# Query projections and attention in one program: gate of three tiles from resident tokens, sampled tokens' attention spread over the chunks

## The reference

```
groups: (window, dilation) = (128, 1), (512, 4), (2048, 16)
query t reads positions t - k*d, k = 0..window/d, that are >= 0
s = q . k * SCALE;  lse = logsumexp(s);  o = exp(s - lse) @ v        per group and head
o = sum over groups of softmax(lses)[group] * o[group]
x = x + RMSNorm_post((o * silu(z)) @ w_out)
```

## Time and profile before

| what | value |
|---|---|
| median of 3 runs | 2730.37 us |
| the profiled execution, its own time | 2728.19 us |
| its span, first to last instruction | 2726.1 us |
| mean granted TensorE clock | 0.969 |
| PE busy | 2594.7 us (95%) |
| DVE, ACT, POOL busy | 1138.7, 856.0, 540.5 us |
| last query matmul starts | 1823.57 us |
| first matmul of the sampled tokens starts | 1851.78 us |
| first score matmul of the prompt starts | 1926.80 us |

### The profile page before, as it was taken

One profiled execution on the slowest core, in us unless ns is written; L12 is line 12 of the kernel. 1 busy time (PEld: TensorE's weight loads), 2 busy tenths in 40 slices (PEclk: granted clock), 3 DMA queues, 4 the chain that ended last, 5 costly groups with the idle time before them and its releaser, 6 DMA issues. The chain is left out here.

```text
span 2726.1 us, 38145 instructions
## 1 busy us (share of the span) xinstructions
PE 2594.7 (95%) x14140; PEld 2379.5 (87%) x14140; DVE 1138.7 (42%) x2431; ACT 856.0 (31%) x2109; POOL 540.5 (20%) x577
## 2 busy tenths in 40 slices
PE   6999999999999979999999999977899999899997
PEld 5999999999988757778999999976799899788885
DVE  7311112111144433211434545431455665677774
ACT  6211111111145432100000000003466666666662
POOL 1010101010012211111222222220222122233332
PEclk9999999999999989999999999995799999899999
DMA  4323333232365543873445455445566565544441
GB/s 156 96 81 96 99 106 93 83 115 94 124 198 186 173 156 125 250 213 110 101 114 119 115 119 120 113 93 165 185 243 236 199 214 193 200 137 152 152 152 64
DMA packets 303428, 391.12 MB, mean 143 GB/s; under 512 B 79261, under 2 KB 228405, under 8 KB 301770
## 3 DMA queue, kind: packets, MB, share of 16 engines
q1 hardware_dynamic: 297114, 345.55, 41.5%
q10 hardware_dynamic: 6192, 44.01, 5.0%
HBM read 269.84 MB, written 163.68 MB: 159 GB/s over the span
## 5 line engine op out<-in xcount | busy, mean ns | idle before, releaser
L281 PE MATMUL a_pair<-a_ht_hi,a_w_hi 128*128 128x412 f32 (+1 forms) x1280 | 448.7, 351 | 2.0 <-DVE a_ht_lo L450 2.0
L282 PE MATMUL a_pair<-a_ht_lo,a_w_hi 128*128 128x412 f32 (+1 forms) x1280 | 447.8, 350 | 0.0
L283 PE MATMUL a_pair<-a_ht_hi,a_w_lo 128*128 128x412 f32 (+1 forms) x1280 | 447.8, 350 | 0.0
L1121 PE MATMUL p_pair<-p_ht_lo,p_q_hi 128*128 128x416 f32 (+1 forms) x960 | 335.5, 350 | 0.0
L1120 PE MATMUL p_pair<-p_ht_hi,p_q_hi 128*128 128x416 f32 (+1 forms) x960 | 335.5, 349 | 0.0
L1122 PE MATMUL p_pair<-p_ht_hi,p_q_lo 128*128 128x416 f32 (+1 forms) x960 | 334.3, 348 | 0.0
L281 PEld LDWEIGHTS a_pair<-a_ht_hi,a_w_hi 128*128 128x128 f32 x1280 | 241.5, 189 | 3.0 <-DVE a_ht_lo L450 2.4
L282 PEld LDWEIGHTS a_pair<-a_ht_lo,a_w_hi 128*128 128x128 f32 x1280 | 241.2, 188 | 1.0
L283 PEld LDWEIGHTS a_pair<-a_ht_hi,a_w_lo 128*128 128x128 f32 x1280 | 241.1, 188 | 0.6
L1304 POOL TENSOR_TENSOR p_q_out<-p_q_out,p_turned 128x416 f32<-128x416 f32 (+1 forms) x120 | 139.3, 1177 | 399.7 <-DVE p_turned L1251 325.8
L1249 DVE TENSOR_TENSOR p_q_out<-p_pair,p_table 128x416 f32<-128x416 f32 (+1 forms) x120 | 93.0, 775 | 293.8 <-PE p_pair L1122 173.9
(11 more groups left out here) (217 smaller groups left out, 5173.7 us busy)
## 6 DMA issues: line engine op xcount, KB each, us to landing
out_cache_kv_g_sample<-cache_kv_g ACTq DMA_DIRECT2D x72, 410.0 KB, 3.6
p_table<-rope_columns SPq DMA_DIRECT2D x60, 416.0 KB, 3.2
scratch_q_tiles<-p_q_out SPq DMA_DIRECT2D x48, 512.0 KB, 5.7
g_q_raw<-scratch_q_tiles SPq DMA_DIRECT2D x48, 512.0 KB, 3.9
scratch_partial<-g_parts SPq DMA_DIRECT2D x32, 520.0 KB, 4.7
g_parts<-scratch_partial SPq DMA_DIRECT2D x32, 520.0 KB, 6.4
a_w_raw<-a_w_in SPq DMA_DIRECT2D x32, 512.0 KB, 6.5
g_rows_hi<-scratch_ht_tiles SPq DMA_DIRECT2D x32, 512.0 KB, 5.6
```

The source lines that it names most:

```text
L281: nc.tensor.matmul(out, hi, ht_hi[:, k, cols], start=(k == 0), stop=False)
L282: nc.tensor.matmul(out, hi, ht_lo[:, k, cols], start=False, stop=False)
L283: last = nc.tensor.matmul(out, lo, ht_hi[:, k, cols], start=False, stop=(k == KT - 1))
L1121: nc.tensor.matmul(out, hi, ht_lo[:, k, cols], start=False, stop=False)
```

## The change

Blocks 2, 3 and 4 become one. `attention_phase` turns into `attention_programs`, which returns pieces that `projection_phase` puts behind its own on each engine; `sample_attention_phase` is gone. In detail:

- The query pairs run from group 2 to group 0 (`q_group`), so the tiles that attention takes first are stored first.
- The first half of the gate weights is loaded and split during the last pair: SP loads slices 0 to 3 ahead of the pair's tables and 4 to 7 between them, ACT makes the high parts, and DVE makes two low parts ahead of each of the first four rotations. The first of these loads waits until the store of pair 10 has landed.
- The gate jobs 0 to 2 (Z_FIRST = 3) read the resident ht_hi and ht_lo and stand right behind the last query job on PE; the turns of keys 0 and 1 stand ahead of job 2.
- Most buffers of attention lie in memory of the projection that is free by then. Keys 0 and 1 lie in that of q_out1, so their load waits for the last store (s_qstore[1]); queries 0 lie in that of the weights and are loaded as soon as the last query job is done (`load_first`).
- The second half of the gate weights is split in chunks 2, 5, ..., 23, the output weights from chunk 29 on. PACE of group 1 falls from 2.36 to 2.0, as there are 24 steps fewer.
- The sampled tokens' attention becomes 33 steps (11 per group) in chunks 4 to 15, 19 to 30 and 34 to 45, one per chunk, ahead of its values. Each writes the bank whose turn it is and is evacuated by DVE. Their caches are loaded by SP ahead of chunk 0 and in the turns of chunks 17 and 32.
- `ident`, `pair`, `tps` are those of the projection: the gate's two banks are pair[0], the value sums pair[1].

```diff
+        def q_group(p):
+            return GROUPS - 1 - p // PAIRS
...
+            load_table(0)
             load_pair(1)
             for p in range(ALL_PAIRS):
+                if p == ALL_PAIRS - 1:
+                    after.load_weights(sp, range(4))
                 for c in range(NCH):
                     if NCH * p + c + 1 < NCH * ALL_PAIRS:
                         load_table(NCH * p + c + 1)
+                    if p == ALL_PAIRS - 1 and c < 2:
+                        after.load_weights(sp, (2 * c + 4, 2 * c + 5))
                 if p + 2 < ALL_PAIRS:
                     load_pair(p + 2)
+                if p == ALL_PAIRS - 1:
+                    after.load_first(sp)
                 store_pair(p)
...
             for p in range(ALL_PAIRS):
+                if p == ALL_PAIRS - 1:
+                    after.halve(dve)
                 for c in range(NCH):
+                    if p == ALL_PAIRS - 1 and c < 4:
+                        after.weights_lo(dve, 2 * c)
+                        after.weights_lo(dve, 2 * c + 1)
                     rotate(p, c)
...
+            if n == 0:
+                sp.wait_ge(s_qstore[0], q_stored)
+            if n >= RAW:
+                sp.wait_ge(s_wlo, n - RAW + 1)
+            sp.dma_start(w_raw[n % RAW][:], w_views[kind][:, k, half * BANK:(half + 1) * BANK])\
+              .then_inc(s_wraw[n % RAW], 16)
...
+        sp.wait_ge(s_q, q_jobs)
+        load_queries(sp, 0)
...
+        all_stored(sp)
+        load_rows(Z_FIRST)
+        load_weights(sp, range(KT, KT + RAW))
+        sp.wait_ge(s_qstore[1], q_stored)
+        load_keys(sp, 0)
+        load_tile(1)
+        store_gate(0)
+        load_tile(2)
+        store_gate(1)
+        load_rows(Z_FIRST + 1)
+        store_gate(2)
+        load_tile(3)
+        load_sample(0)
...
+        for z in range(Z_FIRST):
+            if z == Z_FIRST - 1:
+                turn_keys(0)
+                turn_keys(1)
+            for k in range(KT):
+                gate_step(z, k)
+        scores(0)
+        scores(1)
+        turn_probs(0)
+        scores(2)
...
+            if c in sample_in:
+                sample_step(*sample_in[c])
+            if i > 0 or j is None:
+                values(c)
...
+        queries_hi(0)
+        gate_tanh_of(0)
+        values_hi(0)
+        gate_tanh_of(1)
+        keys_hi(0)
+        keys_hi(1)
+        values_hi(1)
+        queries_hi(1)
+        gate_tanh_of(2)
+        exponentials(0)
...
+    STEPS = ("queries", "keys0", "keys1", "scores0", "keys2", "keys3", "scores1", "score", "prob", "sums", "sum")
+    BEGIN = (4, 19, 34)
+    sample_in = {BEGIN[x] + m + (m >= 8): (x, step) for x in range(GROUPS) for m, step in enumerate(STEPS)}
+    sample_load = {BEGIN[x] + 13: x + 1 for x in range(GROUPS - 1)}
...
+        def sample_step(x, step):
...
+            what = ("sample", x, step)
+            out = bank(*what)
+            bank_free(*what)
...
+            elif step[:6] == "scores":
+                half = int(step[6:])
+                pe.wait_ge(s_lo, turned("sample", x, f"keys{2 * half + 1}"))
+                for y in range(8):
+                    row = (8 * half + y) * QPK
+                    last = nc.tensor.matmul(out[:, row:row + QPK], keys_t[y // 4][:, y % 4, :], s_qt[:, row:row + QPK],
+                                            start=True, stop=True)
```

More of the change, by code:

```diff
@@ L1123, in _ @@
                         last.then_inc(s_q, 1)
+            after.products(pe)
         @block.scalar
@@ L1185, in _ @@
                     split_pair(p, k)
+            for k in range(KT):
+                after.weights_hi(act, k)
+            after.exponentials(act)
         @block.vector
@@ L1279, in _ @@
                         split_pair(p + 1, 2 * c + 1)
+            after.sums(dve)
         @block.gpsimd
@@ new lines, in attention_programs @@
+    wide = [pair[0][:, b, :] for b in range(2)]
+    sums = pair[1][:].rearrange("p a (h c d) -> p (a h) c d", h=QPK // 2, c=2)
+    score = [ctx.enter_context(nc.psum_tensor(f"g_score{b}", [P, BANK], F32)) for b in range(2)]
+    s_gain = sem("gain_landed")
+    s_mask = sem("mask_ready")
+    s_qraw = [sem(f"q_landed{b}") for b in range(2)]
+    s_kvraw = [sem(f"kv_landed{b}") for b in range(2)]
+    s_rows = [sem(f"rows_landed{b}") for b in range(2)]
+    s_wraw = [sem(f"w_landed{b}") for b in range(RAW)]
@@ new lines, in turned, with bank, load_weights @@
+    def turned(*what):
+        return turn_of[what] + 1
+    def bank(*what):
+        return tps[turn_of[what] % 2]
+    def load_weights(sp, ns):
+        for n in ns:
+            kind, half, k = sliced(n)
+            if n == 0:
[4 more added lines that the diff above has]
+              .then_inc(s_wraw[n % RAW], 16)
@@ new lines, in weights_hi @@
+    def weights_hi(act, n):
+        kind, half, k = sliced(n)
+        act.wait_ge(s_wraw[n % RAW], 16 * (n // RAW + 1))
+        if n == 0:
+            act.wait_ge(s_halved, 1)
+            act.wait_ge(s_q, q_jobs * 11 // 12)
+        elif n % KT == 0:
+            act.wait_ge(s_z, (0, Z_FIRST, NT + 1, Z_JOBS)[n // KT])
+        dst = w_hi[half][:, k, :]
+        if kind == "gate":
+            nc.scalar.activation(dst, w_raw[n % RAW][:], ACT.Copy, scale=gains[:, 1, k:k + 1]).then_inc(s_whi, 1)
+        else:
+            nc.scalar.activation(dst, w_raw[n % RAW][:], ACT.Copy).then_inc(s_whi, 1)
@@ new lines, in weigh, with halve, weights_lo @@
+    def weigh(engine, b, g):
+        x = parts[b][:, g, 0:D].rearrange("p (h d) -> p h d", d=HD)
+        return engine.tensor_tensor(x, x, coef[:, 2, g, :].unsqueeze(2).to_broadcast([P, HEADS, HD]), ALU.mult)
+    def halve(dve):
+        dve.wait_ge(s_qsplit, KT * q_jobs // 5)
+        nc.vector.tensor_scalar(gains[:, 1, :], gains[:, 1, :], 0.5, None, ALU.mult).then_inc(s_halved, 1)
+    def weights_lo(dve, n):
+        kind, half, k = sliced(n)
+        if n == 0:
+            dve.wait_ge(s_halved, 1)
+        dve.wait_ge(s_whi, n + 1)
+        dst, high = w_lo[half][:, k, :], w_hi[half][:, k, :].bitcast(F32)
+        if kind == "gate":
+            nc.vector.scalar_tensor_tensor(out=dst, in0=w_raw[n % RAW][:], scalar=gains[:, 1, k:k + 1], in1=high,
+                                           op0=ALU.mult, op1=ALU.subtract).then_inc(s_wlo, 1)
+        else:
+            nc.vector.tensor_tensor(dst, w_raw[n % RAW][:], high, ALU.subtract).then_inc(s_wlo, 1)
```

1960 lines of the change are left out of this document (911 added, 1049 removed).

## The result

The changed kernel takes 2706.93 us (median of four runs, 2705.96 to 2711.18) against 2730.07 us for the kernel before (four runs, 2727.31 to 2730.38): ratio 0.992, 95% interval [0.9908, 0.9933]. It is 23 us faster, not the 51 us of the forecast; the time lies where rival 2 had put it (2700 to 2715). The profiled execution took 2705.96 us, its span 2704.2 us.

What follows compares the result with a forecast made beforehand. TensorE was taken as the bound, with a matmul under way 2594.7 of 2726.1 us. Terms -75.9 (stretch to first values), -16.9 (gate steps), +28 and +3 (sampled tokens), +10 (last query pair) sum to -51.8: about 2679 us, range 2658 to 2708.

Steps and rivals of the forecast that it cites:

- rival 2: Loop loads queue behind 6 MB of caches, last query pair's stall reaches its upper end: 2700 to 2715 us; chance 0.16.
- Part 3: Sampled tokens in the attention loop: 28 us of PE work at full clock, +3 for 33 steps (bounds 0 and +15).
- a clock below 0.9: Chunks 4 to 45: a clock under this level there was named as a sign that the prediction was wrong.
- rival 1: Chunks 4 to 45: clock falls under the sampled steps, up to 2889 us at half clock throughout; chance 0.08.
- that they just fit: Attention loop: cache loads issued two chunks ahead land in 11.8 us, about two chunks; covered by the +15 upper bound.
- At nothing: Changes priced at zero: turned group order, later first table, and splits moved to other chunks with 0.64 and 0.68 us operations.
- Part 1: Last query matmul to first value products' end: 121.9 us become about 46, bounds 40 and 58; gain 75.9 us.
- the nearer case: After the pause for keys 0, clock returns some 7 us after restart, as after 978.14, not 18 us as after 1926.80.
- Part 2: Attention loop: 72 gate matmuls leave it, a gain of 16.9 us, bounds 10 and 17.
- Part 4: Last query pair: PE stalls 7.2 us before the third job, +3 for half clock; taken as +10, bounds 5 and 16.

Runs made afterwards that it cites:

- the last kernel: Changed kernel with five loss-removing edits, a fourth gate tile ahead of the loop, and queries 1 loaded first behind the last store: 2658.49 us, 0.9731 of before.
- value products wide: Against the changed kernel, the sampled value step's 16 products move 64 columns each, not 4 (result not right, times alone): 2701.35 us.
- scores twice: Against the changed kernel, each of the six sampled score steps makes its 8 products of 4 columns twice: 2729.97 us.
- the edit that should remove both: Against the changed kernel, in the last query pair DVE makes two low parts behind each of the first four rotations, not ahead: 2700.61 us.
- these edits: Value step halved, caches behind keys, rotation first, keys early, splits shifted, then a fourth gate tile and queries 1 first, on the changed kernel: 2658.49 us.
- the kernel with the caches behind the keys: Against the changed kernel, first cache half loaded behind the tile load, second two chunks later, sampled queries some four chunks earlier: 2703.49 us.

## Why the prediction was wrong

The direction and the mechanisms of the gain were right; Part 3 failed, and with it the size.

- **Part 3 (forecast +31: 28 of PE work and 3 for the steps).** Chunks 2 to 45 grew by 53.4 us. As cut here, this stage also lost 12 gate products (450 against 462 in the traces) to group 1's slower pace, 2.8 us at 0.235, so the steps cost 56.2 us. PE's work was as forecast: without falls and with 5.7 us of waits these chunks take 251.4 us in the last kernel, against 223.0 - 2.8 + 31 = 251.2. The 25 us beyond it are pauses (15.5 us, where 1.7 of before and 3 forecast make 4.7: 10.8 more) and half clock (16.5 us, less 1.9 inside a pause: 14.6). "The sampled steps at a granted clock of 1.00 with 28 us of PE between chunks 4 and 45 and hardly a wait" is the step that failed. The sign that I had named for it, a clock below 0.9, was too coarse: 0.94 was enough.
- **Against rival 1 I had argued with an average:** the sampled work is an eighth of each chunk, between products of 512 columns. But it isn't spread: a value step is 3.6 us of nothing but 4-column products, and behind it the clock fell. Rival 1 was right about the place and far too dear in price. Its limits are in the runs: the same 16 products cut in two had no fall of their own, nor had they 64 columns wide; 8 products made 16 had one in five cases of six. The rule that I cited with it, from the Trainium skill (TensorE: Matmul & The Clock Gate, A second HAM failure mode: psum-queue depth-cycling), is not what acts at the value steps: the round of the banks was longer in the first case, the same in the others.
- **Rival 2, the loads, was right about the mechanism.** Two chunks ahead isn't early when 2 MB stand in front on the same queue: 7.67 us. I had seen the 11.8 us of a cache load and put "that they just fit" into an upper end. That the time fell in rival 2's range is in part luck: nearly half of the half clock (7.9 of 16.5 us) stands behind the value steps, which rival 2 did not have.
- **"At nothing" for the moved splits was wrong, and so was a price:** the 0.68 us that I took for a low part is another operation's; the low parts had a mean of 1.74 us in before, beside POOL's. That cost nothing there. Here four operations of the sampled score stand behind one, and it cost 2.14 us and a fall; another is one of the two causes of the 1.31 us wait.
- **Part 1 (46 us, bounds 40 and 58): 52.3, mis-sized by 6.3.** The two gate tiles ended at t = 11.2 (11.3 forecast) and the last store landed at 18.4 (17.6). Keys 0 landed at 25.3, not 22.5: issued at 19.4 behind a rows tile (two loads) and four weight slices, they took 5.9 us and not 4.5. The clock came back 7.6 us behind the restart (7 forecast), so the nearer case (the restart at 978.14) was the right one, and the first scores began at 35.7 (33). What I did not have is the second fall, 10.2 us from 1874.0, in the ramp, which took 16.6 us, not 13. It doesn't always come: in two executions with the same code up to here (value products wide, scores twice) the stretch had none and took 48.1 and 48.2 us.
- **Part 2 (-16.9)** came: 2.8 (worked out above), 11.3 and 4.7 us in the three stages are 18.8, for 72 gate products in the traces (12, 45 and 15). The 2 us beyond are not taken apart here.
- **Part 4 (+10) had the right mechanism:** the pause was 6.63 us (7.2 forecast) in the place named, the clock was half for another 3.5 us behind the restart (1.8 us lost), and the edit that should remove both did. Together they are 8.4 us. That the stage is 10.3 us longer is in part luck: in the seven other executions with this pause it was 11.0 to 19.5 us longer, and 3.9 us without it.

Open: what a fall takes at one and the same pause. The 2.14 us in chunk 42 stood in eight executions: three had a fall of 6.8 us there, three one of 20.5 or 23.9, and two none. No run tells that apart, nor why one value step had no fall and why the second fall in the ramp comes and goes.

## What to carry to other kernels

Before work is moved from an idle stretch into a full loop, look at what runs in a row and not at its share: a few microseconds of products with hardly any columns can cost the wide products behind them half their clock, and cutting them in two costs next to nothing. Big loads go behind the small ones that the loop waits for, in halves. The time of an operation is read from its own row, beside the engine that it will meet. Where a stretch has lost one pause, look at the clock in the next: the 48 us that these edits gave came from pauses of 2 to 14 us and from the falls beside them.

## What the runs showed of the hardware

- 16 float32 products took 3.63 us with 4 columns and 3.68 us with 64: at these widths the columns don't set their time, but the clock fell behind the narrow ones alone.
- Of 21 uncut value steps of 4 columns in seven executions (six kernels), 18 had a fall of their own, two stood in one that had begun at a pause, and one had none (the first, in the kernel with the caches behind the keys). So a single profile can show one fall too few.
- The pause for keys behind the caches (6.87 to 8.86 us) had a fall in all eight executions that had it, the 2.14 us one in six of eight. The wait of 1.79 us before the first turn of probabilities was followed by one in six of eight executions of kernels with late keys, and by none in the last kernel.
- In chunks 2 to 45 of the changed kernel DVE's low part of a weight slice took 2.36 to 2.48 us in the eight cases in which it began some 0.5 us behind POOL's low part of a query tile, 1.62 us in one that began 1.35 us behind it, and 0.69 to 0.75 us in the seven that met none.
